# Retention stage of a two-layer backbone kernel: tile records resident in SBUF, scores a step ahead, directions summed in the stage

## The chip, the cores and the metric

The kernel runs on one core of a Trainium2 chip. The metric is the time of one execution on the device in microseconds (us). The engines are named as in the profile: PE (matrix products; PEld its weight loads), DVE (VectorE), ACT (ScalarE), POOL (GpSimd) and SP (SyncE, which here only issues DMAs). Each has its own instruction stream, and they meet through semaphores.

## What is computed

Two layers over 1024 latent and 256 context tokens of width 1024. The change touches the mixer of layer 0 alone: retention in both directions over chunks of 128 tokens, four heads of 128, beside a convolution branch whose normalisation is done in the same stage.

```python
def step(state, qkv):                       # one chunk of 128 tokens, each head
    qc, kc, vc = qkv
    s = jnp.einsum('bhid,bhjd->bhij', qc, kc) * intra
    o = jnp.einsum('bhij,bhjv->bhiv', s, vc) + jnp.einsum('bhid,bhdv->bhiv', qc, state) * xi
    state = state * decay_chunk + jnp.einsum('bhjd,bhjv->bhdv', kc * zeta, vc)
    return state, o
...
oc_f, st_f = retention_chunkwise(qc, kc, vc, lg_f, zero)          # context first
oc_b, st_b = retention_chunkwise(flip(qc), flip(kc), flip(vc), lg_b, zero)
ox_f, _ = retention_chunkwise(qx, kx, vx, lg_f, st_f)             # then the latents
ox_b, _ = retention_chunkwise(flip(qx), flip(kx), flip(vx), lg_b, st_b)
...
ret = head_group_norm(o_f, gn_g) * silu(gf) + head_group_norm(o_b, gn_g) * silu(gb)
conv = conformer_conv(bv, bg, conv_w, conv_b, ln_g, ln_b)
out = concatenate([ret, conv], axis=-1) @ w_out
```

After this come the second norm, an expert-choice mixture (16 experts), and a second layer with latent attention instead of retention.

## The kernel before

The kernel is a chain of stages with a barrier between them: `front` (input projection and convolution), `retention`, `mixer_out` (output projection, norm, router), `routing`, `experts`, then `latents`, `attention`, `mixer_out`, `routing`, `experts` for layer 1. Inside a stage each engine's code is written by hand in order, and semaphores join them; nothing reorders it.

`front` leaves one record per token tile in `rec_d`: turned queries, turned keys, keys, values (128 x 512 fp32 each, so 1 MB) and two gates of 256 KB. Context tiles are stored twice, ahead of and behind the latent ones.

`retention` (L813) runs 10 steps, one tile for each direction d. In step t direction 0 takes record t and direction 1 record 11 - t. One step does, for both directions:

- PE: the scores (L921), a turn of the convolution tile `ys` (L239), keys times values (L932), the outputs (L941 and L942 in turns), a turn of `yn` (L239).
- DVE: mask the scores into `sm` (L978, reads PSUM and SBUF), scale the queries into `qx` (L980, both inputs in SBUF), statistics of the convolution tile (L983, L988), its shift `cnm` (L990), statistics of the outputs (L995, L1000), new state (L1005, PSUM and SBUF), shift `nm` (L1011, SBUF only).
- POOL: reciprocal roots of the convolution tile (L1039, L1043), of each direction (L1047, L1050), the decayed keys `kz` of the next step (L1031), the gate product into `ret` (L1057).
- ACT: `yn` (L1093), the next `ys` (L1086), the normalised outputs `xh` (L1102), the convolution result `mixc` (L1109).
- SP: the records of two steps on (L878, L880) into two buffers per direction, issued when that buffer's gate product is done; then three stores, `mixc` into `mix_d` and the two directions into `ret_f_d` and `ret_b_d` (L892, L897).

All products of a step wait for the step before: `sm`, `qx`, `kz` and `state` have one buffer for each direction. The output weights (4 MB, L869) are loaded ahead of the first record.

`mixer_out` (L1117) takes a tile at a time: SP loads both directions of the tile (L1185, L1186) and the convolution half (L1190), POOL adds the directions (L1351), PE turns the sum, ACT copies it into `mix`, ACT and DVE split `mix` into a high and a low part, PE multiplies (L1254), DVE forms the residual and the norm (L1320 to L1336), PE turns `h` (L239) and routes it (L1277). The first tile also waits for the split weights (L1375, L1378, L1291, L1294); later tiles wait for the rows of modulation (L1308).

Of the kernel before, what the change touches and what calls it, by code (L numbers as in the profile page):

```python
# [25 lines left out]
ALU = mybir.AluOpType  # L26
# [3 lines left out]
P = 128  # L30
# [782 lines left out]
def retention(nc, io, g, conv):  # L813


    with ExitStack() as st:
# [3 lines left out]
        carve = Carve(g.ring, WOUT)  # L820
        rec = [[carve(5 * HALF) for b in range(2)] for d in dirs]
        table = tile("table", [P, 6 * P + 2])
        lg, lga, decay = (tile(n, [P, 2 * HEADS]) for n in ("lg", "lga", "decay"))
        intra = [carve(HALF) for d in dirs]
        xi = [carve(HALF) for d in dirs]
        zeta = tile("zeta", [P, 2 * HEADS])
        state = [carve(HALF) for d in dirs]
        sm = [carve(HALF) for d in dirs]
        qx = [carve(HALF) for d in dirs]
        kz = [carve(HALF) for d in dirs]  # L830
        xh = [carve(HALF) for d in dirs]
        ret = [[tile(f"ret{d}{b}", [P, HALF]) for b in range(2)] for d in dirs]
        stats = [tile(f"stats{d}", [P, HEADS, 6]) for d in dirs]
        mv = [tile(f"mv{d}", [P, HEADS, 2]) for d in dirs]
        ve = [tile(f"ve{d}", [P, HEADS]) for d in dirs]
        rs = [tile(f"rs{d}", [P, HEADS]) for d in dirs]
        nm = [tile(f"nm{d}", [P, HEADS]) for d in dirs]
# [5 lines left out]
        table_in, lg_in, ln_in, setup = sem("table_in"), sem("lg_in"), sem("ln_in"), sem("setup")  # L843
        tables_made = sem("tables_made")
        rec_in = [sem.pair(f"rec_in{d}") for d in dirs]
        ret_out = [sem.pair(f"ret_out{d}") for d in dirs]
        scored = [sem(f"scored{d}") for d in dirs]
        masked = [sem(f"masked{d}") for d in dirs]
        qx_set = [sem(f"qx_set{d}") for d in dirs]
        kz_set = [sem(f"kz_set{d}") for d in dirs]  # L850
        kv_sum = [sem(f"kv_sum{d}") for d in dirs]
        out_sum = [sem(f"out_sum{d}") for d in dirs]
        state_set = [sem(f"state_set{d}") for d in dirs]
        stat = [sem(f"stat{d}") for d in dirs]
        root = [sem(f"root{d}") for d in dirs]
        shift = [sem(f"shift{d}") for d in dirs]
        normed = [sem(f"normed{d}") for d in dirs]
        gated = [sem(f"gated{d}") for d in dirs]
        c_cut, c_turned, c_stat, c_root, c_shift, c_normed, c_back, c_done = (
            sem("c_" + n) for n in ("cut", "turned", "stat", "root", "shift", "normed", "back", "done"))  # L860
        mixc_out = sem.pair("mixc_out")

        with nc.Block() as block:
            @block.sync
            def _(sp):
                sp.dma_start(table[:, :], io["ret_table"]).then_inc(table_in, 16)
                sp.dma_start(lg[:, :], io["ret_logit"].partition_broadcast(P)).then_inc(lg_in, 16)
                sp.dma_start(ln[:, :], io["conv_ln"]).then_inc(ln_in, 16)
                sp.dma_start(g.ring[:, 0:WOUT], io["ev_w_out"]).then_inc(g.wout_in, 16)  # L869
                sp.dma_start(g.router[:, :], io["router_w"][0]).then_inc(g.wout_in, 16)  # L870

                def load(a):
                    for d in dirs:
                        r = a.t if d == 0 else NT + 1 - a.t
                        sp.wait_ge(gated[d], a.t + 1)
                        settle(sp, g)
                        src = rows(io["rec_d"], r)
                        sp.dma_start(rec[d][a.b][:, 0:4 * HALF], src[:, 0:4 * HALF]).then_inc(rec_in[d][a.b], 16)  # L878
                        gcol = (R_GF + d) * HALF
                        sp.dma_start(rec[d][a.b][:, 4 * HALF:], src[:, gcol:gcol + HALF]).then_inc(rec_in[d][a.b], 16)  # L880
                for d in dirs:
                    sp.sem_inc(ret_out[d][0], 16)
                    sp.sem_inc(ret_out[d][1], 16)
                sp.sem_inc(mixc_out[0], 16)
                sp.sem_inc(mixc_out[1], 16)

                def step(a):
                    if a.plus(2).exists(NT):
                        load(a.plus(2))
                    sp.wait_ge(c_done, a.t + 1)  # L890
                    settle(sp, g)
                    sp.dma_start(rows(io["mix_d"], a.t)[:, HALF:D], mixc[a.b][:, :]).then_inc(mixc_out[a.b], 16)  # L892
                    for d in dirs:
                        r = a.t if d == 0 else NT + 1 - a.t
                        sp.wait_ge(gated[d], a.t + 3)
                        settle(sp, g)
                        sp.dma_start(rows(io["ret_d"][d], r), ret[d][a.b][:, :]).then_inc(ret_out[d][a.b], 16)  # L897
                load(At(0, 0))
                load(At(0, 1))
                run(sp, step, NT // 2, 0, NT // 2 - 1)  # L900
                for b in range(2):
                    sp.wait_ge(mixc_out[b], 16 * (NT // 2 + 1))
                    for d in dirs:
                        sp.wait_ge(ret_out[d][b], 16 * (NT // 2 + 1))

            @block.tensor
            def _(pe):
                for d in dirs:
                    pe.sem_inc(kv_sum[d], 1)
                    pe.sem_inc(out_sum[d], 1)  # L910

                def hs(x, h, at=0):
                    return x[:, at + h * HD:at + (h + 1) * HD]
# [1745 lines left out]
```

## Time and profile before

| | |
|---|---|
| three runs | 3379.59, 3380.14 (median), 3390.08 us |
| profiled execution | 3382.69 us, its span 3380.9 us |
| PE, DVE, ACT, POOL busy | 2924.2, 2080.8, 1409.5, 520.6 us |
| retention, first DMA to that of the next stage | 513.3 to 673.1 us |
| mixer_out of layer 0 | 673.1 to 856.5 us |
| mean granted TensorE clock | 0.935 of full speed |

The page shows shares of the whole span. The touched stage is 160 us of 3381, so it is read from the timeline, from the busy time by stretch, and from the waits inside it. A row of the timeline gives start, duration, engine, line, operation, output and inputs, and in brackets the idle time before it with what ended it.

### The profile page before, as it was taken

To read this page: it belongs to the slowest core of one execution; us is meant where nothing else is said; L and a number is where in the kernel's file an instruction comes from. 1 tells how busy PE (TensorE), PEld (TensorE's weight loads), DVE (VectorE), ACT (ScalarE), POOL (GpSimd) and SP (SyncE) were. 2 spreads that over 40 slices of the span, in tenths; PEclk is the share of its full clock that TensorE was granted. 3 is DMA by queue.
4 is the path that set the end of the run, shared out by engine and by line. 5 is a ranking of instruction groups with operands and counts; after the bars stand their busy time and mean duration, and the time that the engine had idled before them with its cause. 6 is when DMAs were issued, how large, how long until landed. Compare 5 with 4: busy or idle time off the path is not lost. (4 is left out here: it accounts for less than half of the span.)

```text
span 3380.9 us, 51489 instructions
## 1 busy us (share of the span) xinstructions
PE 2924.2 (86%) x19792; PEld 2312.1 (68%) x19792; DVE 2080.8 (62%) x2164; ACT 1409.5 (42%) x1717; POOL 520.6 (15%) x487
## 2 busy tenths in 40 slices
PE   6999995688099999999949997799997819999998
PEld 3766785667078888888835554688886708777776
DVE  3577825654766666666712232566664488888887
ACT  2212114432055555555512334344332217777675
POOL 0000004511012122212214446000000001111111
PEclk8999997899599999999979999899998959999999
DMA  5368616653467788778641223522203349999995
GB/s 214 125 211 267 218 60 250 221 184 128 171 224 279 284 308 283 280 284 304 222 167 45 69 66 95 157 81 61 70 21 112 119 183 359 377 375 373 370 378 174
DMA packets 160338, 690.25 MB, mean 204 GB/s; under 512 B 14337, under 2 KB 78849, under 8 KB 124514
## 3 DMA queue, kind: packets, MB, share of 16 engines
q1 hardware_dynamic: 145634, 650.97, 52.8%
q0 software_dynamic: 14592, 37.76, 4.7%
q8 instruction: 73, 1.20, 0.1%
q14 instruction: 39, 0.32, 0.0%
HBM read 600.50 MB, written 88.18 MB: 204 GB/s over the span
## 5 line engine op out<-in xcount | busy, mean ns | idle before, releaser
L1784 DVE TENSOR_TENSOR ex_wlo<-ring,ex_whi 128x2048 fp32r<-128x2048 f32 x384 | 877.2, 2289 | 264.9 <-ACT ex_whi L1711 260.8
L1711 ACT CAST ex_whi<-ring 128x2048 fp32r<-128x2048 f32 x384 | 727.5, 1905 | 251.1 <-PE psum L1676 250.8
L1676 PE MATMUL psum<-ex_whi,ex_xh 128*128 128x512 f32 x1024 | 411.4, 402 | 10.8 <-DVE ex_wlo L1784 10.8
L1676 PE MATMUL psum<-ex_wlo,ex_xh 128*128 128x512 f32 x1024 | 401.2, 392 | 0.0
L1676 PE MATMUL psum<-ex_whi,ex_xl 128*128 128x512 f32 x1024 | 400.8, 391 | 0.0
L1676 PEld LDWEIGHTS psum<-ex_whi,ex_xh 128*128 128x128 f32 x1024 | 193.5, 189 | 61.6 <-DVE ex_wlo L1784 14.8
L529 PE MATMUL psum<-fr_whi,fr_hh 128*128 128x512 f32 x560 | 223.8, 401 | 12.9 <-DVE fr_hl L713 11.5
L1676 PEld LDWEIGHTS psum<-ex_whi,ex_xl 128*128 128x128 f32 x1024 | 193.4, 189 | 41.8
L1676 PEld LDWEIGHTS psum<-ex_wlo,ex_xh 128*128 128x128 f32 x1024 | 193.7, 189 | 37.2
L529 PE MATMUL psum<-fr_wlo,fr_hh 128*128 128x512 f32 x560 | 218.1, 391 | 0.7 <-DVE fr_wlo L719 0.7
L529 PE MATMUL psum<-fr_whi,fr_hl 128*128 128x512 f32 x560 | 218.1, 391 | 0.0
L1676 PE MATMUL psum<-ex_whi,ex_hh 128*128 128x512 f32 x512 | 211.1, 412 | 0.0
L1676 PE MATMUL psum<-ex_whi,ex_hl 128*128 128x512 f32 x512 | 202.2, 395 | 0.0
L1676 PE MATMUL psum<-ex_wlo,ex_hh 128*128 128x512 f32 x512 | 201.9, 394 | 0.0
L774 DVE SCALAR_TENSOR_TENSOR conv_y<-conv_u,fr_taps,conv_y 128x1295 f32<-128x1295 f32 x120 | 180.0, 1560 | 0.0
L2438 PE MATMUL psum<-ring 128*128 128x128 f32 x1280 | 161.5, 282 | 7.2 <-DVE ring L2450 6.0
L2438 PEld LDWEIGHTS psum<-ring 128*128 128x128 f32 x1280 | 149.4, 193 | 18.2 <-DVE ring L2450 13.9
L2034 PE MATMUL psum<-ring,la_cT 128*128 128x384 f32 (+1 forms) x416 | 154.0, 530 | 0.6 <-ACT la_cT L2108 0.6
L1574 POOL DMA_INDIRECT x_d<-ring,idx_x x16 | 52.5, 3281 | 608.4 <-DVE ring L1822 608.4
L239 PE MATMUL psum<-ident,ring 128*128 128x128 f32 x440 | 64.9, 294 | 82.2 <-DMA ring<-h_d,idx_x 39.4
L529 PEld LDWEIGHTS psum<-fr_whi,fr_hh 128*128 128x128 f32 x560 | 105.6, 189 | 40.9 <-DVE fr_hl L713 11.9
L1254 PE MATMUL psum<-mo_w_high,mo_mix_high 128*128 128x512 f32 x288 | 118.2, 410 | 17.7 <-DVE mo_mix_low L1299 17.7
(278 smaller groups left out, 5235.8 us busy)
## 6 DMA issues: line engine op xcount, KB each, us to landing
ring<-in_moe_w SPq DMA_DIRECT2D x192, 2048.0 KB, 9.8
fr_raw<-in_mod_w SPq DMA_DIRECT2D x40, 1024.0 KB, 5.7
ring<-rec_d SPq DMA_DIRECT2D x20, 1024.0 KB, 7.1
rec_d<-fr_work SPq DMA_DIRECT2D x72, 256.0 KB, 5.8
fr_raw<-in_ev_w_in SPq DMA_DIRECT2D x14, 1024.0 KB, 5.6
h_d<-ring SPq DMA_DIRECT2D x18, 512.0 KB, 3.0
fr_arena<-in_mod_w SPq DMA_DIRECT2D x8, 1024.0 KB, 13.8
ring<-mod_d SPq DMA_DIRECT2D x11, 512.0 KB
```

Source lines behind the costliest of these rows:

```text
L239: last = nc.tensor.transpose(g.psum[:, bank + n // 4, (n % 4) * P:(n % 4 + 1) * P], src[:, k * P:(k + 1) * P], g.ident[:, :])
L529: last = nc.tensor.matmul(g.psum[:, bank(s), :], pairs[n][0][t][:, 4 * b + k, :], pairs[n][1][m % 3][:, k, :], start=(b == 0 and i == 0), ...
L774: nc.vector.scalar_tensor_tensor(conv.y[:, j, :], us, w, conv.y[:, j, :], ALU.mult, ALU.add).then_inc(conv_set[j], 1)
L1254: last = nc.tensor.matmul(g.psum[:, 1 + 2 * a.b + c, :], x_part[a.b][:, k * P:(k + 1) * P], w_part[:, k, c * BANK:(c + 1) * BANK], start=( ...
L1574: pool.indirect_dma_start(dst, bass.IndirectOffsetOnAxis(ap=idx[:, e:e + 1], axis=0), src[:, :], None, compute_op=ALU.add).then_inc(done, 16)
L1676: last = nc.tensor.matmul(g.psum[:, 2 + i % 2, :], x[:, 4 * b + k, :], w[n][:, k, :], start=(b == 0 and k == 0 and first == 0), stop=(b == ...
L1711: nc.scalar.copy(whi[m % RING][:, :, :], slot(i)[:, 4 * b:4 * b + 4, :]).then_inc(hi_set, 1)
L1784: nc.vector.tensor_tensor(wlo[n][:, :, :], slot(i)[:, 4 * b:4 * b + 4, :], whi[n][:, :, :].bitcast(F32), ALU.subtract).then_inc(lo_set, 1)
L2034: last = nc.tensor.matmul(g.psum[:, 6 + m % 2, 0:width], cT[:, (k0 + k) * P:(k0 + k + 1) * P], w[:, k, c0:c0 + width], start=(k == 0), sto ...
L2438: last = nc.tensor.matmul(g.psum[:, 7, 0:P], v[mu // per_head_units][:, k, :], pT[:, k * P:(k + 1) * P], start=(k == 0), stop=(k == KEYT - 1))
```

## The change

- The records of all ten tiles stay in the ring, 1 MB each, loaded once; context records serve both directions. Only gates are still double buffered (L872), freed by the gate product. They fill the first 10 MB of the 14 MB ring, so the output weights' place is taken by the first four slots, and the weights come in two halves of 2 MB, after steps 2 and 7 (L898 to L905), when those tiles are finished in both directions.
- `sm`, `qx` and `state` have two buffers. The masked scores of step i + 1 are made at the head of step i on DVE, and PE computes scores i + 1 ahead of everything else of step i.
- On DVE the state update moves ahead of the statistics; the shift of direction 1 moves into the next step. On ACT direction 1 is normalised at the head of the next step. On POOL the gate products follow a step behind, and the decayed keys come before the roots of the directions.
- The gate product of the direction that reaches a tile first is written into `total`; the other multiplies in place (L1084) and adds (L1088). `total` lies where the convolution input was. One store per tile goes to `mix_d`. In `mixer_out` the two loads and the add become one load (L1250).
- The loops are written out, so branches, tick increments and register waits go; SP loads `re_lg` ahead of the table.

```diff
+        order = [[XT, XT + 1] + list(range(XT)), [XT + 1, XT] + list(reversed(range(XT)))]
+        slots = [8, 9, 3, 4, 0, 7, 1, 6, 2, 5]
+        rec = {t: g.ring[:, n * TREC:(n + 1) * TREC] for n, t in enumerate(slots)}
+        total = [uf[:, t * HALF:(t + 1) * HALF] for t in range(NT)]
+        def second(i):
+
+            return i == 1 or i >= 2 + XT // 2
...
+                for i in range(2, 2 + XT // 2):
+                    for d in dirs:
+                        load_rec(order[d][i])
...
+                    if i == 2:
+                        for d in dirs:
+                            sp.wait_ge(out_sum[d], 2)
+                        load_wout(0)
...
+                for i in range(NT):
+                    if i + 1 < NT:
+                        for d in dirs:
+                            scores(i + 1, d)
...
+                def gated_output(i, d):
+                    b, t = i % 2, order[d][i]
+                    pool.wait_ge(normed[d], i + 1)
+                    pool.wait_ge(gate_in[d][b], 16 * (i // 2 + 1))
+                    if not second(i):
+                        nc.gpsimd.tensor_tensor(total[t], xh[d][:, :], gate[d][b], ALU.mult).then_inc(gated[d], 1)
+                        return
+                    nc.gpsimd.tensor_tensor(xh[d][:, :], xh[d][:, :], gate[d][b], ALU.mult).then_inc(gated[d], 1)
...
+                    nc.gpsimd.tensor_tensor(total[t], total[t], xh[d][:, :], ALU.add).then_inc(added[d], 1)
...
-                        rt = a.t - XT if a.stream() else a.t + CT
-                        sp.dma_start(rf[b], rows(io["ret_d"][0], rt)).then_inc(r_in[b], 16)
-                        sp.dma_start(rb[b], rows(io["ret_d"][1], a.t + CT)).then_inc(r_in[b], 16)
+                        sp.dma_start(ret[b], rows(io["mix_d"], a.t)[:, 0:HALF]).then_inc(r_in[b], 16)
...
-                def add(a):
-                    pool.wait_ge(r_in[a.b], 32 * (a.i + 1))
-                    pool.wait_ge(r_turned, a.t + 1)
-                    nc.gpsimd.tensor_tensor(rsum, rf[a.b], rb[a.b], ALU.add).then_inc(r_sum, 1)
```

DVE, one step of retention before: masks, convolution statistics, output statistics, state, with a shift behind each state.

```order
180 L978 TENSOR_TENSOR ring<-psum,ring 128x512
181 L980 TENSOR_TENSOR ring<-ring 128x512
182 L978 TENSOR_TENSOR ring<-psum,ring 128x512
183 L980 TENSOR_TENSOR ring<-ring 128x512
184 L983 BN_STATS re_cst<-psum 128x6
185 L988 BN_AGGR re_cmv<-re_cst 128x2
186 L990 SCALAR_TENSOR_TENSOR re_cnm<-re_cmv,re_crs 128x1
187 L995 BN_STATS re_stats<-psum 128x6 x4
188 L1000 BN_AGGR re_mv<-re_stats 128x2 x4
```

DVE, after, from the shift of direction 0 that closes one step: the masks that follow serve the outputs of the step after the one they stand in; the second shift belongs to the step just closed.

```order
197 L1032 SCALAR_TENSOR_TENSOR re_nm<-re_mv,re_rs 128x4
198 L1001 TENSOR_TENSOR ring<-psum,ring 128x512
199 L1002 TENSOR_TENSOR re_qx<-ring 128x512
200 L1032 SCALAR_TENSOR_TENSOR re_nm<-re_mv,re_rs 128x4
201 L1001 TENSOR_TENSOR ring<-psum,ring 128x512
202 L1002 TENSOR_TENSOR re_qx<-ring 128x512
203 L1044 BN_STATS re_cst<-psum 128x6
204 L1048 BN_AGGR re_cmv<-re_cst 128x2
205 L1012 SCALAR_TENSOR_TENSOR re_state<-re_state,re_decay,psum 128x128 x4
206 L1054 SCALAR_TENSOR_TENSOR re_cnm<-re_cmv,re_crs 128x1
207 L1012 SCALAR_TENSOR_TENSOR re_state<-re_state,re_decay,psum 128x128 x4
```

The masks moved a step ahead, a state update came between the statistics and `cnm`, and the output statistics moved to the step's end.

POOL, one step before: roots of the directions, then keys, then both gate products.

```order
47 L1050 TENSOR_TENSOR re_rs<-re_ve,mhalf 128x4
48 L1047 TENSOR_SCALAR re_ve<-re_mv 128x4
49 L1050 TENSOR_TENSOR re_rs<-re_ve,mhalf 128x4
50 L1031 TENSOR_TENSOR ring<-ring,re_zeta 128x512 x2
51 L1057 TENSOR_TENSOR re_ret<-ring 128x512 x2
```

POOL, one step after in which the tiles are met for the second time (L1084 the product, L1088 the add).

```order
99 L1084 TENSOR_TENSOR ring<-ring 128x512
100 L1088 TENSOR_TENSOR conv_u<-conv_u,ring 128x512
101 L1109 TENSOR_SCALAR re_cve<-re_cmv 128x1
102 L1113 TENSOR_TENSOR re_crs<-re_cve,mhalf 128x1
103 L1073 TENSOR_TENSOR ring<-ring,re_zeta 128x512 x2
104 L1084 TENSOR_TENSOR ring<-ring 128x512
105 L1088 TENSOR_TENSOR conv_u<-conv_u,ring 128x512
```

The keys now follow the convolution's root at once, and one gate product lies on each side of them; the roots of the directions come last.

## Rows read from the trace of the kernel before

**Rows 1.** Busy time by stretch, from one `cnm` to the next. Columns: stretch, length, PE, PEld, DVE, ACT, POOL (instructions), clock, DMA share, GB/s.
```profile
540.08:552.53 12.45, 11.05 (x98) 10.78 (x97) 9.18 (x34) 7.08 (x15) 8.72 (x10) 1.00 0.12 34
...
552.53:565.89 13.36, 8.37 (x47) 7.76 (x47) 9.21 (x33) 5.70 (x14) 7.83 (x10) 0.74 0.82 289
...
sum 118.11, PE 88.91 PEld 85.30 DVE 82.96 ACT 52.41 POOL 75.03; mean PE 9.88 PEld 9.48 DVE 9.22 ACT 5.82 POOL 8.34
```

**Rows 2.** Groups of instructions, 540 to 660 us: busy, mean ns, idle before.
```profile
L921 PE MATMUL psum<-ring 128*128 128x128 f32 x144 | 25.1, 330 | 26.6 <-DMA ring<-rec_d 26.6
```

**Rows 3.** Timeline of one step, ACT, POOL and DVE, 623 to 631 us.
```profile
623.53 1.03 POOL L1050 TENSOR_TENSOR re_rs<-re_ve,mhalf 128x4 f32<-128x4 f32 x1
623.94 0.15 DVE L1011 SCALAR_TENSOR_TENSOR re_nm<-re_mv,re_rs 128x4 f32<-128x4 f32 x1
...
624.13 3.00 ACT L1102 ACTIVATE ring<-psum,re_nm,re_rs 128x128 f32<-128x128 f32 x8 [3.46 <-DVE re_nm L1011]
624.53 2.15 POOL L1031 TENSOR_TENSOR ring<-ring,re_zeta 128x512 f32<-128x512 f32 x2
625.05 0.54 DVE L1011 SCALAR_TENSOR_TENSOR re_nm<-re_mv,re_rs 128x4 f32<-128x4 f32 x1
...
626.64 3.40 POOL L1057 TENSOR_TENSOR re_ret<-ring 128x512 f32<-128x512 f32 x2
...
630.43 0.58 POOL L1043 TENSOR_TENSOR re_crs<-re_cve,mhalf 128x1 f32<-128x1 f32 x1
```

**Rows 4.** Line L980 (`qx`) in the whole stage: duration ns least, median, most.
```profile
L980 DVE TENSOR_TENSOR ring<-ring x20: 680/888/1459, 534.2 to 654.7; 128x512 f32<-128x512 f32 x20
```

**Rows 5.** Timeline of the stage's start, DVE, PE and POOL.
```profile
526.69 1.29 DVE L968 TENSOR_TENSOR ring<-ring,re_table 128x512 f32<-128x512 f32 x2 [6.22 <-ACT re_decay L1078]
...
531.46 2.07 PE L921 MATMUL psum<-ring 128*128 128x128 f32 x8 [22.88 <-DMA ring<-rec_d]
...
543.34 1.05 POOL L1050 TENSOR_TENSOR re_rs<-re_ve,mhalf 128x4 f32<-128x4 f32 x1
```

**Rows 6.** Timeline of PE: keys times values at either clock, outputs, turn.
```profile
640.05 1.95 PE L932 MATMUL psum<-ring 128*128 128x128 f32 x16
...
641.84 0.39 PE L941 MATMUL psum<-ring 128*128 128x128 f32 x2
...
645.41 0.60 PE L239 MATMUL psum<-ident,re_yn 128*128 128x128 f32 x4
...
654.74 3.23 PE L932 MATMUL psum<-ring 128*128 128x128 f32 x16
```

**Rows 7.** Timeline of the stage's end, POOL and SP's queue.
```profile
663.51 1.04 POOL L1050 TENSOR_TENSOR re_rs<-re_ve,mhalf 128x4 f32<-128x4 f32 x1
...
665.70 2.67 POOL L1057 TENSOR_TENSOR re_ret<-ring 128x512 f32<-128x512 f32 x2 [1.16 <-ACT ring L1102]
...
669.42 0.39 SPq L897 DMA_DIRECT2D ret_b_d<-re_ret  x1
673.10 0.35 SPq L1173 DMA_DIRECT2D mo_gn<-in_ret_gn_g  x1
```

**Rows 8.** Timeline in `mixer_out`, DVE and POOL.
```profile
693.66 2.36 DVE L1308 SCALAR_TENSOR_TENSOR ring<-ring 128x1024 f32<-128x1024 f32 x2 [4.21 <-DMA ring<-in_norm_g]
...
703.67 1.29 POOL L1351 TENSOR_TENSOR ring<-ring 128x512 f32<-128x512 f32 x1
703.74 2.30 DVE L1333 SCALAR_TENSOR_TENSOR ring<-ring,mo_rstd 128x1024 f32<-128x1024 f32 x1 [2.25 <-POOL mo_rstd L1362]
...
830.11 1.29 DVE L1333 SCALAR_TENSOR_TENSOR ring<-ring,mo_rstd 128x1024 f32<-128x1024 f32 x1 [2.15 <-POOL mo_rstd L1362]
```

**Rows 9.** Timeline of PE in `mixer_out`: turns of `h` for tiles 7 and 8.
```profile
818.23 1.09 PE L239 MATMUL psum<-ident,ring 128*128 128x128 f32 x8 [1.11 <-DVE ring L1336]
...
832.71 1.09 PE L239 MATMUL psum<-ident,ring 128*128 128x128 f32 x8
```

**Rows 10.** Waits, 700 to 860 us: us in total, times, longest.
```profile
PE psum L239 <- DVE ring L1336: 16.8, 9, 5.7
```

More of the change, by code:

```diff
@@ new lines, in scores @@
+                def scores(i, d):
+                    r = rec[order[d][i]]
+                    pe.wait_ge(rec_in[order[d][i]], 16)
+                    if i:
+                        pe.wait_ge(masked[d], i)
+                    for h in range(HEADS):
+                        last = nc.tensor.matmul(g.psum[:, d, h * P:(h + 1) * P], hs(r, h, R_KT * HALF),
+                                                hs(r, h, R_QT * HALF), start=True, stop=True)
+                    last.then_inc(scored[d], 1)
@@ new lines, in update @@
+                def update(i, d):
+                    dve.wait_ge(kv_sum[d], i + 1)
+                    if i:
+                        dve.wait_ge(out_sum[d], i)
+                    dve.wait_ge(state_set[d], i + 1)
+                    for h in range(HEADS):
+                        c = slice(h * P, (h + 1) * P)
+                        last = nc.vector.scalar_tensor_tensor(state[d][(i + 1) % 2][:, c], state[d][i % 2][:, c],
+                                                              decay[:, d * HEADS + h:d * HEADS + h + 1],
+                                                              g.psum[:, 2 + d, c], ALU.mult, ALU.add)
+                    last.then_inc(state_set[d], 1)
@@ new lines, in moments @@
+                def moments(i, d):
+                    dve.wait_ge(out_sum[d], i + 1)
+                    if i:
+                        dve.wait_ge(root[d], 2 * i - 1)
+                        dve.wait_ge(shift[d], i)
+                    for h in range(HEADS):
+                        nc.vector.bn_stats(stats[d][:, h, :], g.psum[:, 4 + d, h * P:(h + 1) * P]).then_inc(stat[d], 1)
+                    dve.wait_ge(stat[d], 2 * HEADS * i + HEADS)
+                    for h in range(HEADS):
+                        nc.vector.bn_aggr(mv[d][:, h, :], stats[d][:, h, :]).then_inc(stat[d], 1)
@@ L971, in _, with shifted @@
+                def shifted(i, d):
+                    dve.wait_ge(root[d], 2 * i + 2)
+                    if i:
+                        dve.wait_ge(normed[d], i)
+                    nc.vector.scalar_tensor_tensor(nm[d][:, :], mv[d][:, :, 0], -1.0, rs[d][:, :],
+                                                   ALU.mult, ALU.mult).then_inc(shift[d], 1)
                 for d in dirs:
-                    dve.sem_inc(masked[d], 1)
-                def step(a):
+                    mask(0, d)
@@ new lines, in normalise @@
+                def normalise(i, d):
+                    act.wait_ge(shift[d], i + 1)
+                    if i:
+                        act.wait_ge(gated[d], i)
+                        if second(i - 1):
+                            act.wait_ge(added[d], seconds(i - 1))
+                    for h in range(HEADS):
+                        c = slice(h * P, (h + 1) * P)
+                        last = nc.scalar.activation(xh[d][:, c], g.psum[:, 4 + d, c], ACT.Identity,
+                                                    bias=nm[d][:, h:h + 1], scale=rs[d][:, h:h + 1])
+                    last.then_inc(normed[d], 1)
```

400 lines of the change are left out of this document (189 added, 211 removed).

## The prediction

> **What bounds the kernel now.** The stages follow each other behind barriers, so the question is what retention (513.3 to 673.1 us) and the `mixer_out` behind it (to 856.5) cost; nothing after them starts earlier by itself, and what is gained there shortens the whole. I read first the busy time from one `cnm` to the next [rows 1]: nine steps take 118.1 us, 13.1 each, while PE is busy 9.9, DVE 9.2, POOL 8.3 and ACT 5.8. No engine is full. Then the waits: PE waits for records 26.6 us in nine steps, 3.0 each [rows 2]. But the first stretch, which moves next to nothing by DMA, still takes 12.45 us [rows 1]. So the records explain some 0.7 to 3 us of a step, and a ring of dependent work the rest: roots on POOL, shift on DVE, eight normalisations on ACT (3.00 us), and only then outputs, keys and gate products [rows 3]. Its order, more than its content, is what the change alters.
>
> A third thing is to be seen there. An operation of DVE with two inputs in SBUF is held up by a POOL operation on 512 columns: the shift `nm` takes 0.15 us alone and 0.54 beside `kz`, ending when the first `kz` does [rows 3]; `qx` takes 0.68 to 1.46 us [rows 4]; and in `mixer_out` L1333 takes 2.30 us when POOL's add starts 0.07 ahead of it, 1.29 without an add [rows 8]. Beside POOL's root (L1050) the shift kept its 0.15 [rows 3].
>
> **The change, part by part.**
>
> *Retention, a step without adds.* I count from the end of the root of direction 0 on POOL (0.0). DVE: shift at 0.0, first mask with `qx` to 1.5, shift of direction 1 to 1.65 (POOL's second root takes 1.4), second `sm` to 2.3. ACT has direction 0 normalised at 1.75 (half of 3.00), so POOL's gate product starts at 2.0 and holds the second `qx` until 3.3: it ends at 3.9. Convolution statistics to 4.9, POOL's root of them to 6.0 (0.58 for the power [rows 3]). POOL goes on to `kz` without a gap, and `cnm`, with two SBUF inputs, loses to it as L1333 lost to the add, which followed a root in the same way [rows 8]: `cnm` ends at 7.1. One state update has run meanwhile, the other ends at 8.2, the statistics of direction 0 at 9.6, POOL's sum and root 1.5 later. A step is thus 11.2 us. As a check on DVE's busy time: 9.2 [rows 1], less 0.4 of the held `nm` and 0.4 to 0.6 of two `qx` (median 0.89, least 0.68 [rows 4]), is 8.3; about 0.75 of small waits between dependent operations (an estimate), 1.05 for the second `qx`, 0.9 for `cnm` and 0.2 until the root give 11.2.
>
> The other engines have room. PE at full clock needs 1.95 for the scores, as many columns as L932, 1.95 for keys, 3.6 for the outputs (641.84 to 645.41) and two turns of about 0.5 [rows 6]: 8.5 us, waiting some 2.5. POOL has 8.3, ACT 5.8 [rows 1]. The records: 10.5 MB of records and 1 MB of gates are loaded at the rate at which the start already loads, some 400 GB/s; the pair for step 2 is there more than 10 us ahead. So the 3.0 us of waits [rows 2] go to nothing, and what is late next is DVE.
>
> *Steps with adds.* The add runs in steps 2, 7, 8, 9 and the tail, for both directions. An add is like L1351, 1.29 us [rows 8]; the L1057 product is 1.25 to 1.7 [rows 3, 7]. In steps 2 and 7 POOL is the last: gates 2.0 to 4.7, 0.6 given to `qx`, root 0.9, keys 2.1 (2.15 [rows 3]), gates 2.7, root 1.35, in all 12.3. Step 8 makes no keys: 11.5. Step 9 has no mask, no state: 9.9. Sum: five steps of 11.2 (1, 3 to 6), 2 x 12.3, 11.5, 9.9: **102.0 us**. Before, from the first root's end (544.39 [rows 5]) to the same point of step 9 (its direction 0 ended at about 662.7, 0.8 ahead of the second's start at 663.51 [rows 7]) it was 118.3.
>
> *The start.* The masks wait for `intra`, which ended at 527.98 [rows 5]; its logits are loaded 0.4 earlier now, so 527.6. Before, the first scores waited for a record until 531.46 [rows 5], since 4 MB of weights went first. Now they are ready. From 527.6: first mask 0.7; scores of step 1 at half clock, 2.07 each [rows 5], the second pair from the second mask (530.1), to 532.3; turn 1.0; keys 3.2 at half clock [rows 6] to 536.6; outputs of direction 0 to 538.6; statistics and root 3.2: 541.8. Before it was 544.4: **2.5 us** gained.
>
> *The tail.* Before, the store that ended last was issued at 669.42 and the next stage's first DMA at 673.10, 3.7 later [rows 7]. Now both gate products with adds stand behind the last roots: root of direction 1 to 1.4, products and adds 1.9 to 7.1. So 541.8 + 102.0 = 643.8, + 7.1 + 0.1 + 3.7 = 654.7. Against 673.1 retention gains **18.4 us**. The weights are there: their second half is issued after step 7, over 25 us ahead of use, and 2 MB are some 5 us of DMA. Gates are asked for a whole step early.
>
> *mixer_out.* Two loads and an add leave each tile. The add had no place on the path by itself, but it holds L1333: 2.30 against 1.29 [rows 8], 1.01 us in each of eight tiles, and PE then waits for L1336 behind it, 16.8 us in 9 waits, one of 5.7 in the last tile, so 11.1 in the other eight, the least 1.1 [rows 9, 10]. Each wait is longer than what DVE saves, so all of 8 x 1.01 = **8.1 us** comes off. The tile after the last add took 14.5 us with PE waiting for nothing [rows 9]; that is the floor. At the start, the rows of modulation and the norm's gain, landed at 693.66 [rows 8], hold tile 1; 0.5 MB less lies ahead of them, **1.3 us**. Bounds: 0 and 10.
>
> All in all 18.4 + 8.1 + 1.3 = 27.8 us. The profiled execution took 3382.7 (span 3380.9): 3354.9. It was 2.6 above the median of the runs, which I take as the scatter of runs; against the median, **3352**.
>
> **A rule weighed.** The Trainium skill, SBUF — State Buffer, "Who interferes with whom", says that a DVE instruction with two SBUF inputs and a POOL instruction that reads SBUF exclude each other for the whole instruction, the first to start winning. The L1333 and `nm` rows agree. It would also hold `nm` beside POOL's root, which also reads SBUF; there the row has 0.15, so the measurement decides.
>
> **Rivals.**
>
> *A, ports dearer.* If the roots also hold DVE, the first `qx` waits from 0.9 to 1.4, and POOL, held in turn, slips as L1057 does (1.70 a piece beside `qx`, 1.33 later [rows 3, 7]): 0.5 to 1.0 more a step. Or the steps stay at the 12.45 that a step without DMA took [rows 1]: 9 x 12.45 = 112, 10 more, 3362. For: DVE and POOL overlap more than before. Against: the order is another.
>
> *B, ports cheaper.* If `cnm` and `qx` win their races, 1.95 a step goes where DVE is last, six steps: 12 less, but POOL's own round (first gate product from 2.0, root, keys, second product, root) then closes the step at about 10, so 8 or 9 less: 3343.
>
> *C, the clock, slower than before.* At the stage's start the scores run at half speed, and in steps of 13.4 us with a waiting PE the mean granted clock was 0.74 [rows 1]. Keys then cost 3.23 instead of 1.95 [rows 6]; at that ratio PE needs 8.5 x 1.66 = 14.1, with turns and waits some 16, in every step: nine steps 144 us, 42 more, 3394. It decides from 14.3 us a step, where the gain of 28 is spent. For: the stretch of 552.53 had it in part. Against: it fell when PE had waited for records, and stayed at 1.00 through the stretch with PE busy 11.05 of 12.45 [rows 1]; now it is about 8.5 of 11.2.
>
> *D, the change brings the records but not the rest.* If the ring of POOL, DVE and ACT closes as before and the add's removal is taken up by another wait, only 2.5 at the start and about 1 a step of waits remain, less 2 in the tail: 3371.
>
> **How the numbers follow.** Forecast (3346 to 3358) 0.55; A at its far end 0.17; B 0.13; D 0.08; C 0.05; anything else 0.02. The range is 3340 to 3367: it leaves out C, D and the rest, and takes in B and A with a few us for the mixer's bound. A measurement of this kernel can tell about 0.3%, 10 us, from no change. Below 3370: forecast, A, B and part of D, 0.89. Within: the rest of D, 0.05. Slower: C and half of the rest, 0.06.
>
> **What would show it.** Right: `cnm` to `cnm` of 11.2 us, and 12.3 in steps 2 and 7; no PE wait for `rec_d` after the first scores; `cnm` at about 1 us instead of 0.16 behind L1113; `qx` of direction 1 at 1.5; L1333's successor at 1.29 in all tiles, mixer tiles of 14.5; the stage's length 141 us. Wrong: steps of 12.5 with POOL full say A; 10 with `cnm` at 0.16 says B; a clock near 0.5 in mid-stage says C; a new PE wait in `mixer_out`, for the copied sum or the split, says that the 8.1 was not free. A wait for a gate or for the weights would break the sum at a place where I gave nothing.

## The result, and the profile after

The changed kernel takes 3348.23 us (median of five runs, 3343.91 to 3358.16) against 3380.14 us for the kernel before (five runs, 3377.04 to 3390.08): ratio 0.9903, 95% interval 0.988 to 0.9926. The forecast of 3352 (3340 to 3367) held. Its profiled execution took 3348.23 us, span 3344.6, against 3382.69 and 3380.9. That the total lay so near is partly luck: in the traces the two stages gained 11 us more than forecast, and 7 us of that gain is not seen in the medians. So the result is laid out by stage.

| profiled execution, us | before | after | difference | forecast |
|---|---|---|---|---|
| all ahead of retention | 513.3 | 512.1 | -1.3 | 0 |
| retention, first DMA to the next stage's | 159.8 | 131.2 | -28.6 | -18.4 |
| mixer_out of layer 0 | 183.4 | 172.9 | -10.5 | -9.4 |
| all behind it | 2524.4 | 2528.5 | +4.1 | 0 |

Busy time by stretch in the kernel after, from one `cnm` to the next, as [rows 1]. Columns: stretch, length, PE, PEld, DVE, ACT, POOL (instructions), clock, DMA share, GB/s.

```profile
565.98:576.12 10.14, 8.48 (x74) 8.12 (x73) 9.70 (x35) 5.73 (x14) 7.84 (x11) 1.00 0.61 204
576.12:586.36 10.24, 8.57 (x74) 8.14 (x73) 9.75 (x34) 5.73 (x14) 7.93 (x11) 1.00 0.24 79
...
606.84:618.61 11.77, 9.88 (x72) 9.69 (x72) 9.72 (x33) 5.73 (x14) 10.72 (x13) 0.86 0.60 204
...
sum 95.11, PE 76.34 PEld 73.56 DVE 83.44 ACT 52.71 POOL 77.20; mean PE 8.48 PEld 8.17 DVE 9.27 ACT 5.86 POOL 8.58
```

Nine steps take 95.1 us where they took 118.1. DVE's busy time is what it was, 9.3 a step; the step has closed up around it. PE waits for a record only ahead of the first scores (waits of 510 to 660 us: total, times, longest), where [rows 2] had 26.6 us inside the steps.

```profile
PE psum L930 <- DMA ring<-rec_d: 12.9, 2, 12.5
```

The start, PE's timeline. The first scores run at half clock as in [rows 5], but start 7.7 us after the stage's first DMA instead of 18.1. The granted clock had risen when the keys came: L938 takes 1.95 us, where the forecast had 3.2.

```profile
519.81 2.08 PE L930 MATMUL psum<-ring 128*128 128x128 f32 x8 [12.49 <-DMA ring<-rec_d]
522.34 2.02 PE L930 MATMUL psum<-ring 128*128 128x128 f32 x8 [0.46 <-DMA ring<-rec_d]
527.07 3.59 PE L930 MATMUL psum<-ring 128*128 128x128 f32 x16 [2.71 <-DVE ring L1001]
...
531.17 1.95 PE L938 MATMUL psum<-ring 128*128 128x128 f32 x16
```

The end, SP's queue, as [rows 7]: the tail from the root of direction 0 in the last step (632.90) to the next stage is 10.3 us, as before.

```profile
637.48 2.89 SPq L917 DMA_DIRECT2D mix_d<-conv_u  x2
643.23 0.35 SPq L1239 DMA_DIRECT2D mo_gn<-in_ret_gn_g  x1
```

`mixer_out`: L1397 (L1333 before) at all its 18 places, least, median and most in ns; PE's first product and three turns of `h`; PE's waits for the line behind L1397 (L1400, L1336 before), 650 to 818 us.

```profile
L1397 DVE SCALAR_TENSOR_TENSOR ring<-ring,mo_rstd x18: 1283/1284/1286, 673.7 to 2659.2; 128x1024 f32<-128x1024 f32 x18
```
```profile
653.19 0.79 PE L1318 MATMUL psum<-mo_w_high,mo_mix_high 128*128 128x512 f32 x1 [5.39 <-DVE mo_mix_low L1363]
...
690.66 1.09 PE L239 MATMUL psum<-ident,ring 128*128 128x128 f32 x8
...
705.24 1.09 PE L239 MATMUL psum<-ident,ring 128*128 128x128 f32 x8 [0.18 <-DVE ring L1400]
...
719.72 1.09 PE L239 MATMUL psum<-ident,ring 128*128 128x128 f32 x8
```
```profile
PE psum L239 <- DVE ring L1400: 7.6, 5, 5.7
```

Nothing holds L1397 any more, the tiles are 14.5 us apart, and of the 16.8 us of waits in [rows 10] the last tile's 5.7 and little more are left. The first product comes 9.96 us after the stage's first DMA, before 12.0, but that brings little: the rows of modulation that tile 1 waits for (L1372, L1308 before) are used 20.4 us after the first DMA instead of 20.6, and the first L1397 starts at 30.5 instead of 30.6.

### The profile page after: what moved, and what is told of

The parts are those of the page before. It is cut to its first block and busy times, and to the rows that moved or that the text cites. A ratio compares the mean times of both kernels' runs of the same rounds, so it can differ in the third digit from the quotient of the medians.

```text
span 3344.6 us, 51073 instructions
## 1 busy us (share of the span) xinstructions
PE 2917.5 (87%) x19776; PEld 2305.3 (69%) x19776; DVE 2074.1 (62%) x2156; ACT 1409.5 (42%) x1717; POOL 513.8 (15%) x485
## 5 line engine op out<-in xcount | busy, mean ns | idle before, releaser
L1731 PE MATMUL psum<-ex_whi,ex_xh 128*128 128x512 f32 x1024 | 410.8, 401 | 10.8 <-DVE ex_wlo L1839 10.8
L1629 POOL DMA_INDIRECT out_x<-ring,idx_x x16 | 52.3, 3271 | 513.8 <-DVE ring L1877 513.8
```

The costliest lines, as they stand in the source:

```text
L1629: pool.indirect_dma_start(dst, bass.IndirectOffsetOnAxis(ap=idx[:, e:e + 1], axis=0), src[:, :], None, compute_op=ALU.add).then_inc(done, 16)
L1731: last = nc.tensor.matmul(g.psum[:, 2 + i % 2, :], x[:, 4 * b + k, :], w[n][:, k, :], start=(b == 0 and k == 0 and first == 0), stop=(b == ...
```

## A step read from the other end

The forecast read steps from one `cnm` to the next and found 12.45 us in a stretch with little DMA [rows 1]. From the end of one root of direction 0 (L1050) to the next, the same trace of the kernel before reads differently:

```profile
544.39:555.55 11.16, 7.82 (x65) 7.12 (x64) 9.44 (x39) 7.08 (x15) 8.69 (x10) 1.00 0.40 138
555.55:570.54 14.99, 11.95 (x80) 11.69 (x80) 8.94 (x30) 5.69 (x14) 7.84 (x10) 0.77 0.84 284
570.54:581.75 11.21, 7.73 (x66) 7.18 (x64) 9.47 (x39) 5.60 (x14) 8.69 (x10) 1.00 0.66 234
581.75:597.55 15.80, 13.08 (x80) 12.72 (x80) 8.94 (x31) 5.70 (x14) 7.83 (x10) 0.68 0.80 273
```

Short and long steps alternate. In the long ones PE waits twice for records (1.57 and 2.81 us, then 1.88 and 2.22) and its clock falls; in the third line it still waits once, 2.01 us; in the first it waits for none. The nine steps took 11.16, 14.99, 11.21, 15.80, 11.23, 13.99, 12.65, 11.69 and 15.64 us. So the old order was good for about 11.2 us, not 12.45; without any wait for records it takes 10.8, as the first experiment shows. The stretch of 12.45 us began in the start-up step: its part up to the root took 4.31 us, with PE busy throughout, where the next one took 3.02. The experiments below use this measure ("root to root").

## The experiments

**Records resident, order as before.** The kernel before with resident records, gates in buffers of their own, the weights in two halves and the loops written out. Its order on every engine, its single buffers, its two stores, and the loads and the add of `mixer_out` stay.

```diff
-        rec = [[carve(5 * HALF) for b in range(2)] for d in dirs]
+        slots = [8, 9, 3, 4, 0, 7, 1, 6, 2, 5]
+        store = {t: g.ring[:, n * TREC:(n + 1) * TREC] for n, t in enumerate(slots)}
+        gate = [[carve(HALF) for b in range(2)] for d in dirs]
...
-                sp.dma_start(g.ring[:, 0:WOUT], io["ev_w_out"]).then_inc(g.wout_in, 16)
...
+                load_rec(XT)
+                load_rec(XT + 1)
+                load(At(0, 0))
+                load(At(0, 1))
+                for t in (0, 7, 1, 6, 2, 5, 3, 4):
+                    load_rec(t)
```

> The kernel before with only the records resident: all ten loaded once, the output weights in two halves behind them, the retention loops written out; order of work on every engine, single buffers, two stores, the add in mixer_out as before. Theory (the gain of a step comes from the order as well as from the loads): the steps fall from 13.1 us only to about 12.0 to 12.4, the wait for records to nothing, the start gains 4; the stage goes from 159.8 to about 147, and the kernel gains 11 to 13 us of the 32. Rival (record loads were the cost): steps of 10.2 to 10.6, the stage at about 133.

Median 3362.51 us (3358.41 to 3366.63, four runs), ratio 0.9928 (0.991 to 0.9946). The stage takes 133.1 us (513.02 to 646.10), `mixer_out` 183.1. So 26.7 of the 28.6 us that retention gained are here, without the new order. The expectation (steps of 12.0 to 12.4, a stage of 147) missed; its rival was right on the stage. Root to root, two of the eight steps that took 10.8:

```profile
560.46:571.27 10.81, 8.60 (x74) 8.14 (x74) 9.09 (x34) 5.69 (x14) 8.68 (x10) 1.00 0.39 134
571.27:582.09 10.82, 8.62 (x75) 8.16 (x74) 9.10 (x34) 5.69 (x14) 8.69 (x10) 1.00 0.90 306
```

Nine steps take 97.7 us (118.4 before, 94.4 in the changed kernel). The second line loads at 306 GB/s and is no longer than the first. The rest of the change to the stage (order, second buffers, the sum made in the stage, one store) is worth 3.3 us in nine steps, and gives back 1.0 at the start (first root 26.4 us after the stage's first DMA, here 25.5) and 0.4 in the tail.

**Loops written out, nothing else.** The kernel before with all ten steps of the stage written out. The cut shows SP; the other four engines have the same edit.

```diff
-                run(sp, step, NT // 2, 0, NT // 2 - 1)
+                run(sp, step, NT // 2, NT // 2, 0)
```

> The kernel before with the retention loops written out and nothing else. Theory (branches, ticks and register waits cost a little in every step): DVE's and POOL's hand-offs inside a step shrink, steps of 12.4 to 12.8 us instead of 13.1, the stage 3 to 6 us shorter than 159.8. Rival (they lie beside other work): 13.0 to 13.2.

One run, 3394.88 us; the stage takes 156.6, 3.2 less. The first step, which waits for no record, takes 11.15 us (11.16 before), and the third, in which PE waits once, 11.17 (11.21 before):

```profile
578.31:589.48 11.17, 7.73 (x66) 7.18 (x64) 9.45 (x39) 5.68 (x14) 8.69 (x10) 1.00 0.63 224
```

So ticks and branches cost at most 0.05 us a step. The 3.2 us lie in the start (0.6) and in the steps that wait longer for records, whose pattern differs between the two traces. The whole is longer than before because in this execution what stands ahead of the stage took 521.6 us instead of 513.3, and what stands behind `mixer_out` 2531.3 instead of 2524.4.

**Output weights behind the first records.** The kernel before with one load moved.

```diff
-                sp.dma_start(g.ring[:, 0:WOUT], io["ev_w_out"]).then_inc(g.wout_in, 16)
-                sp.dma_start(g.router[:, :], io["router_w"][0]).then_inc(g.wout_in, 16)
...
                 load(At(0, 0))
                 load(At(0, 1))
+                sp.dma_start(g.ring[:, 0:WOUT], io["ev_w_out"]).then_inc(g.wout_in, 16)
+                sp.dma_start(g.router[:, :], io["router_w"][0]).then_inc(g.wout_in, 16)
```

> The kernel before, with the load of the output weights and of the router issued behind the records of steps 0 and 1 instead of ahead of them. Theory (the 5.6 us that the start gained with resident records come from the first scores not waiting behind 4 MB): first root of direction 0 ends 25.5 to 27 us after the stage's first DMA instead of 31.05; the nine steps stay at 116 to 120, the stage at 154 to 156 instead of 159.8. Rival (the gain comes from the records' own number or from the order): 30 to 31 at the first root, stage 159 to 160.

One run, 3370.76 us. The first root ends 25.7 us after the first DMA instead of 31.05, the nine steps stay at 117.9, and the stage takes 154.0, 5.8 less. PE waits for no record any more; both scores start right behind DVE's tables, which end at 525.19:

```profile
525.40 3.75 PE L920 MATMUL psum<-ring 128*128 128x128 f32 x16 [19.48 <-DVEq L971]
```

This settles the start: the 4 MB ahead of the first record cost 5.4 us, which two moved lines give back. The nine steps shorten by the other 20.7 us only when the records are resident.

**The hold of `cnm`.** In the changed kernel `cnm` takes 0.89 to 1.21 us beside the keys, where it took 0.16. Here its second input is a scalar for each partition.

```diff
-                    nc.vector.scalar_tensor_tensor(cnm[:, :], cmv[:, 0:1], -1.0, crs[:, :],
-                                                   ALU.mult, ALU.mult).then_inc(c_shift, 1)
+                    nc.vector.tensor_scalar(cnm[:, :], cmv[:, 0:1], crs[:, 0:1], -1.0,
+                                            ALU.mult, ALU.mult).then_inc(c_shift, 1)
```

> The changed kernel with one edit: cnm is made by a tensor_scalar that takes the root as a scalar, so it has one tensor input in SBUF instead of two. Theory (the operation with two inputs in SBUF is held by POOL's first key product): cnm takes 0.16 us instead of 0.99, and each step in which DVE is last shortens by about 0.8 us, from 10.2 to 9.4; in steps 2 and 7, where POOL is last, nothing. Six steps: the stage 131 us minus some 5. Rival (cnm is long because the root's result arrives late): it stays at about 1 us and the steps at 10.2.

One run, 3362.26 us. The hold is gone:

```profile
L1054 DVE TENSOR_SCALAR re_cnm<-re_cmv,re_crs x10: 206/214/214, 543.4 to 636.9; 128x1 f32<-128x1 f32 x10
```

Root to root stays at 10.10 us (10.14 in the changed kernel), the stage takes 129.7 instead of 131.2, of which 0.9 are step 8, where no keys are made. So the hold, 0.8 us on DVE in each step, had slack to stand in, and the 5 us expected from its removal did not come. Only in step 8 (10.67 us, here 9.74) does it cost: there POOL has no keys to make, and in the changed kernel waits 0.99 us for DVE's statistics. What closes the other steps is seen on POOL:

```profile
594.27 0.23 POOL L1109 TENSOR_SCALAR re_cve<-re_cmv 128x1 f32<-128x1 f32 x1 [1.46 <-DVE re_cmv L1048]
594.59 0.58 POOL L1113 TENSOR_TENSOR re_crs<-re_cve,mhalf 128x1 f32<-128x1 f32 x1
595.13 2.04 POOL L1073 TENSOR_TENSOR ring<-ring,re_zeta 128x512 f32<-128x512 f32 x2
...
597.13 1.28 POOL L1082 TENSOR_TENSOR conv_u<-ring 128x512 f32<-128x512 f32 x1
...
598.49 0.23 POOL L1094 TENSOR_SCALAR re_ve<-re_mv 128x4 f32<-128x4 f32 x1
...
598.80 1.03 POOL L1098 TENSOR_TENSOR re_rs<-re_ve,mhalf 128x4 f32<-128x4 f32 x1
```

POOL waits 1.46 us for the convolution statistics, then works without a gap to the root, 5.56 us. DVE takes 4.4 us from the root before (589.76) to the statistics' end (594.18). 4.4 + 5.6 is the step, a ring through both engines, and the held `qx` (1.49 us) stands in DVE's part of it. DVE ended the statistics of direction 0 at 597.75 and the root began only at 598.49, behind the gate product.

**Both second holds.** The same, and `qx` of direction 1 right behind that of direction 0, ahead of the second shift.

```diff
+                    if d == 0:
+                        scaled_queries(i, 0)
+                        scaled_queries(i, 1)
```

> The changed kernel with cnm from a tensor_scalar (one tensor input in SBUF) and the second qx ahead of the second shift and mask, so that it runs before POOL's gate product starts. Theory (two held operations cost 0.8 and 0.9 us a step where DVE is last): qx 0.68 in all places, cnm 0.16, steps from 10.2 to about 9.1 to 9.4 until POOL's own round is last, steps 2 and 7 at about 11; the stage 6 to 9 us shorter than 131.2, the kernel 0.2 to 0.3% faster than the changed one. Rival (another wait is right behind): less than 2 us.

Median 3354.01 us (3347.81 to 3358.36, four runs), ratio 0.9909 (0.9893 to 0.9926). `qx` is free, two in 1.28 us, but now the shift `nm` behind it meets the gate product, and PE no longer gets its masks sooner. Two lines of DVE:

```profile
582.73 1.28 DVE L1011 TENSOR_TENSOR re_qx<-ring 128x512 f32<-128x512 f32 x2
583.93 1.23 DVE L1041 SCALAR_TENSOR_TENSOR re_nm<-re_mv,re_rs 128x4 f32<-128x4 f32 x1
```

Root to root 10.20 us, the stage 130.6; the expected 6 to 9 us did not come, and the rival (less than 2) was right. Here the hold only moved to the next operation with two inputs in SBUF. The convolution statistics still end about 4.5 us after the root, and the step is as long.

**The convolution statistics earlier.** If the ring is DVE's way to these statistics and then POOL's row, it must shorten when they move. First with the one-input `cnm`, then with `cnm` as in the changed kernel:

```diff
                         if d == 0 and i:
                             shifted(i - 1, 1)
+                        if d == 0:
+                            dve.wait_ge(c_turned, i + 1)
+                            nc.vector.bn_stats(cst[:, :], g.psum[:, 6, :]).then_inc(c_stat, 1)
...
+                            nc.vector.bn_aggr(cmv[:, :], cst[:, :]).then_inc(c_stat, 1)
```

> The changed kernel with cnm of one SBUF tensor input, and with the statistics of the convolution tile taken between the two masks of the step instead of behind both. Theory (the step closes through POOL: convolution statistics on DVE at +4.4, then root, keys, the second gate product and the root of direction 0 in a row on POOL, 5.6 us, so 10.1 in all, and DVE's own ring is only 9.1): root to root 9.1 to 9.4 us in steps without adds instead of 10.1, 10.8 to 11 in steps 2 and 7 instead of 11.75 (POOL is then busy without a gap), stage 122 to 125 us instead of 129.7 in the kernel with one-input cnm alone. Rival (DVE's or PE's own ring closes the step): root to root stays at 10.1 and the stage at 129 to 131.

> The same move of the statistics, but cnm with its two SBUF inputs as in the changed kernel. Theory (the hold of cnm by the keys cost nothing where it stood, since DVE had slack, and costs as soon as DVE's ring closes the step): root to root 9.7 to 10.0 us, about 0.6 more than with the one-input cnm; if the hold is never on the ring, the same 9.1 to 9.4 as there; if the statistics' place is not what closes the step, 10.1.

With one-input `cnm`: median 3346.94 us (3337.49 to 3355.97, five runs), ratio 0.989 (0.9861 to 0.992). Root to root 9.04 us, the stage 125.1, so the ring was the right one. With the held `cnm` (one run, 3353.83): 9.08, the stage 127.1; 0.9 of these 2.0 us are step 8 again. The first kernel's lines, a step without adds and step 7, and two of the operations in the former:

```profile
583.67:592.69 9.02, 8.42 (x74) 8.10 (x73) 8.03 (x33) 5.72 (x14) 8.14 (x10) 1.00 0.28 89
601.73:613.47 11.74, 9.76 (x84) 9.22 (x82) 8.12 (x33) 5.71 (x14) 10.69 (x12) 1.00 0.35 106
```
```profile
585.47 1.27 POOL L1083 TENSOR_TENSOR conv_u<-ring 128x512 f32<-128x512 f32 x1 [0.39 <-ACT ring L1158]
...
586.61 0.68 DVE L1002 TENSOR_TENSOR re_qx<-ring 128x512 f32<-128x512 f32 x1
```

POOL no longer waits for the convolution statistics (1.46 us before); from this gate product it works without a gap up to the root at 592.69. The 9.04 us are POOL's own round, with only 0.39 of waiting for ACT. The move did two things at once. It took the second mask and `qx` from in front of the statistics, and it freed that `qx`: it starts 0.13 us before POOL's product ends and takes 0.68 instead of 1.49 us. What each is worth was not tested apart.

Two expectations missed. Steps 2 and 7 did not move: POOL's 10.69 us of work, about 0.08 of hand-off behind each operation and 0.39 of waiting for ACT are already 11.74. And outside step 8 the held `cnm` costs next to nothing still (0.81 here), since POOL reaches the root of direction 0 just as DVE has the statistics (592.63):

```profile
591.32 1.27 POOL L1083 TENSOR_TENSOR conv_u<-ring 128x512 f32<-128x512 f32 x1
592.72 0.23 POOL L1095 TENSOR_SCALAR re_ve<-re_mv 128x4 f32<-128x4 f32 x1
```

**An add, or a fill, in `mixer_out`.** The changed kernel with an addition on POOL of the size and place of the one removed, whose result nobody uses, and the same with a fill of that tile.

```diff
+                    if even and a.plus(1).exists(nt):
+                        pool.wait_ge(a_made, streams)
+                        nc.gpsimd.tensor_tensor(extra, arow[0][:, 0:HALF], arow[0][:, HALF:D], ALU.add)
```
```diff
+                        nc.gpsimd.memset(extra, 0.0)
```

> The changed kernel with an add of 128x512 put back on POOL in mixer_out at the place of the old one; nobody waits for its result and it reads rows that are there anyway. Theory (the old add cost by holding DVE's operation with two inputs in SBUF): that operation takes 2.30 us again in the tiles with an add instead of 1.28, PE waits 1.1 us or more for the turn of h, mixer_out grows by 8 us from 172.9 to 181. Rival (the gain came from the load and the shorter chain of add and turn): it stays at 172.9.

> As the run with the add put back, but the POOL operation is a fill of 128x512, which reads nothing from SBUF. Theory (only POOL operations that read SBUF hold DVE): DVE's operation keeps 1.28 us and mixer_out 172.9. Rival (any POOL operation of that size holds it, or POOL's time itself counts): 2.0 us or more and mixer_out 178 or more.

With the add (one run, 3362.95 us) `mixer_out` takes 182.5, with the fill (one run, 3353.44) 172.7, in the changed kernel 172.9. POOL and DVE, with the add and with the fill:

```profile
707.00 1.29 POOL L1416 TENSOR_TENSOR ring<-ring 128x512 f32<-128x512 f32 x1
```
```profile
707.07 2.30 DVE L1398 SCALAR_TENSOR_TENSOR ring<-ring,mo_rstd 128x1024 f32<-128x1024 f32 x1 [2.15 <-POOL mo_rstd L1423]
```
```profile
706.02 0.53 POOL L1416 MEMSET ring<- 128x512 f32 x1
```
```profile
706.11 1.28 DVE L1398 SCALAR_TENSOR_TENSOR ring<-ring,mo_rstd 128x1024 f32<-128x1024 f32 x1 [2.16 <-POOL mo_rstd L1423]
```

```profile
L1398 DVE SCALAR_TENSOR_TENSOR ring<-ring,mo_rstd 128x1024 f32<-128x1024 f32 x10 | 21.0, 2100 | 21.6 <-POOL mo_rstd L1423 21.6
```

The last line is the group of L1398 in the kernel with the add, ten of 2.10 us on the mean, 8.2 us more than the 12.8 without it. The add alone, with nobody waiting for its result, costs 9.6 us, and PE's waits behind L1401 return to 16.1 (7.7 with the fill). The fill starts at the same place ahead of L1398, overlaps it, and holds nothing.

The 9.6 us are not all hold. From the first L1398 to the second, the kernel with the add takes 16.98 us at a mean granted clock of 0.90, with PE busy for 14.55; the one with the fill 14.38 us at 1.00, with PE busy for 12.92. So 1.6 us of this interval are PE at the lower clock: behind the add PE had waited 2.43 us for L1401, behind the fill 1.46, and then its products came 0.43 us apart instead of 0.23 for a while. The later seven intervals are each about 1.0 us longer. The drop does not always follow: in the kernel before it is there (16.98 us, 0.90), in the one with the weights behind the first records, which also has the add, it is not (15.40 us, 1.00), and that kernel's `mixer_out` takes 181.2 us instead of 183.4.

**The changed kernel again.**

> The changed kernel once more, beside the others of this call. Retention 131.2 us and mixer_out 172.9 as before, to 0.3 us; the stretch behind mixer_out (2528.5 us, 4 more than in the trace of the kernel before) moves by some us from run to run if it is scatter, and stays 4 above that of the kernel before if the change caused it.

Median 3356.48 us (3339.97 to 3364.72, four runs), ratio 0.992 (0.9897 to 0.9944). Stage 131.5 and `mixer_out` 172.6: both repeat within 0.4 us. The kernels with the add and the fill, whose retention is the same, have 132.0 and 132.4 for the stage, so up to 1.2 us between two stages is scatter; root to root repeats within 0.03 us in steps 2 to 9. What stands ahead (510.9) and behind (2521.9) does not repeat. Over the twelve traces the part ahead takes 510.7 to 521.9 us. The part behind takes 2523.1 to 2531.3 in the four kernels with the old order and the old `mixer_out` (mean 2526.5), and 2521.9 to 2534.5 in the other eight (mean 2530.4). The ranges overlap, but the means are 4 us apart, and in routing and experts of layer 0 alone the two groups do not meet (867.6 to 868.2 us against 868.3 to 869.6). The +4.1 of the table is 0.5 in routing and experts, 2.3 in latents, 3.3 in attention with its `mixer_out`, and -2.0 in the last stretch; in this second trace latents and attention are within 1.1 us of the kernel before.

## Why the prediction was right, and where it was wrong

- **Loads off the path: right in kind, its size too small.** The waits went to nothing. The step that failed is "the records explain some 0.7 to 3 us of a step, and a ring of dependent work the rest. Its order, more than its content, is what the change alters". Its first half holds: residency took 20.7 us from nine steps, 2.3 a step. Its second half fails: residency without the order gives 26.7 of 28.6 us, all the rest of the change 1.9, and the old ring of dependent work takes 10.8 us, not 12.45. The cause was the measure: the stretch of 12.45 us between two `cnm` lay across the start-up step and the first full one. The result is in one respect rival D: loads bring nearly all. But D's price for them, "about 1 a step", was 2.3.
- **A step without adds: 11.2 forecast, 10.14 measured,** five steps, 5.2 us. `cnm` (0.99) and the second `qx` (1.49) were held as said, each 0.8 us above its free time (the terms were 0.9 and 1.05). Mis-sized were DVE's busy time, 10.25 by the forecast's terms and 9.70 measured, and its idle time, 0.95 (with the "0.75 of small waits", an estimate with no row) and 0.44 measured. DVE's state updates were to end at 8.2 and the statistics of direction 0 at 9.6 after the root; they ended at 7.5 and 8.7. And "what is late next is DVE" is only half right: DVE sets when POOL's row starts, at 4.5 us, but at the step's end the root of direction 0 stands behind POOL's gate product as much as behind DVE's statistics. One step of the changed kernel, POOL and DVE:

```profile
580.82 0.16 DVE L1032 SCALAR_TENSOR_TENSOR re_nm<-re_mv,re_rs 128x4 f32<-128x4 f32 x1 [0.28 <-POOL re_rs L1098]
...
581.18 1.03 POOL L1098 TENSOR_TENSOR re_rs<-re_ve,mhalf 128x4 f32<-128x4 f32 x1
581.51 0.68 DVE L1002 TENSOR_TENSOR re_qx<-ring 128x512 f32<-128x512 f32 x1
...
582.93 1.49 DVE L1002 TENSOR_TENSOR re_qx<-ring 128x512 f32<-128x512 f32 x1
...
585.07 0.18 DVE L1048 BATCH_NORM_AGGREGATE re_cmv<-re_cst 128x2 f32<-128x6 f32 x1
...
586.36 0.89 DVE L1054 SCALAR_TENSOR_TENSOR re_cnm<-re_cmv,re_crs 128x1 f32<-128x1 f32 x1
...
588.19 1.27 POOL L1082 TENSOR_TENSOR conv_u<-ring 128x512 f32<-128x512 f32 x1
...
589.11 0.38 DVE L1026 BATCH_NORM_AGGREGATE re_mv<-re_stats 128x2 f32<-128x6 f32 x4
...
589.58 0.23 POOL L1094 TENSOR_SCALAR re_ve<-re_mv 128x4 f32<-128x4 f32 x1
```

  The statistics end at 589.49, POOL's product at 589.46: a tie, so taking 0.8 from DVE left 10.10. Rival B's number, a step of about 10, came true, but not its reason: `cnm` and `qx` lost their races. The 10.1 us are a ring, 4.5 us of DVE with the held `qx` in it and 5.7 of POOL; POOL's own round, once it no longer waited for the convolution statistics, took 9.04.
- **Steps with adds: 12.3 forecast, 11.74 and 11.75 measured.** POOL closes them, as said; the 0.6 was given to a held POOL that lost only 0.3. Step 8 took 10.67 (11.5), step 9 9.41 (9.9). All nine: 94.4 against 102.0.
- **The start: 2.5 forecast, 4.6 measured.** The mechanism was right, shown with the weights moved alone. The size missed because keys were priced at half clock (3.2 instead of 1.95) and turns with them.
- **The tail: 10.9 forecast, 10.3 measured.** As before the change.
- **The clock (rival C).** It stayed at 1.00 in every stretch up to step 7, then 0.86 and 0.72 in the last two, and the steps there were no longer for it: POOL closed them. In the kernel before it had been 0.68 to 0.87 in the five steps of 12.6 us and more, in which PE waited for records, and 1.00 in the four shorter ones.
- **mixer_out: 9.4 forecast, 10.5 measured.** The add put back costs 9.6 us. The hold is the 8.2 by which L1398 grows in all, as forecast (8.1). The term of 1.3 for the start failed: the rows of modulation were used 0.2 us earlier, and the first L1397 started 0.2 us earlier. In its place stand 1.6 us of PE at the lower clock in the first interval, which the forecast did not have, and 0.4 in the second; with them the number came out near.
- **The rule weighed.** It holds for `cnm`, `qx` and L1398 in these runs, and the forecast was right to set it aside beside POOL's root. In the changed kernel `nm` no longer meets that root, but `qx` of direction 0 does: in all nine steps it starts 0.3 us after L1098, lies inside its 1.03 us, and keeps 0.68 us. So the premise of rival A, that roots hold DVE too, did not come true.
- **The total.** The stages gained 39.1 us in the traces, 11 more than the 27.8 forecast. The medians differ by 31.9 and, in the second comparison, 28.0. So 7 to 11 us of what the stages gained is not seen in the medians. Parts that the change does not touch scatter by 10 us from run to run, and that alone could explain it. But the mean of the part behind is 4 us longer in the eight traces of changed kernels than in the four others, so some of it may be a lasting loss; the cause was not looked for. Against the sum by stage the forecast was too low, and its total lay near by luck, since it had neither the extra gain of the stages nor the loss in the medians.

## What to carry to other kernels

Measure a pipeline's step between two ends of the same operation on the engine that closes it, and look at each step apart: a mean over alternating 11 and 15 us hid that waits for loads were nearly the whole case. A held operation costs only what sticks out of the ring that closes the step; find that ring by the engine that works without a gap up to the closing operation, and move what starts its row. Freeing a held operation inside the ring may bring nothing when the next one is held in its place. For an engine's add that nobody waits for, ask which operation of the neighbour it holds.

The best version found is the changed kernel with the convolution statistics between the masks and a one-input `cnm`: 6.1 us less in retention than the changed kernel by the traces, at a median of 3346.94 us too near to 3348.23 and 3356.48 to be told apart by the medians. Steps 2 and 7 are then POOL's alone.

## What the runs showed of the hardware

- An operation on one column, `cnm`, 0.16 us alone, was held to 0.89 to 1.21 us beside POOL's 128 x 512 product when it read two tensors in SBUF; as a `tensor_scalar` whose second operand is a scalar for each partition it took 0.21 us in the same place. The Trainium skill, SBUF — State Buffer, "Who interferes with whom", speaks of instructions with two SBUF inputs; the runs show that this scalar does not count as one.
- POOL's fill of 128 x 512, 0.53 us, held L1398 not at all (1.28); the add of the same size did (2.30).
- Statistics of a PSUM tile and the state update, which reads PSUM and SBUF, ran beside POOL's products unheld. In the kernel with the statistics moved, the statistics (L1045) took 0.69 us beside the gate product, and 0.69 in the kernel with one-input `cnm` alone, where they lie clear of it; the state update (L1012) took 1.11 us for four beside the keys, and 1.11 ahead of them.
- POOL's root of 128 x 4 (L1098, 1.03 us), which reads SBUF, did not hold `qx` of 128 x 512, which has two inputs in SBUF and started 0.3 us later: 0.68 us in nine steps of nine.
- In these rows the hold cost the later starter only: POOL's product kept its 1.27 to 1.28 us while `qx` was held, and POOL's `re_cve`, started 0.2 us after a `qx`, was held to 0.55 instead of 0.23 us in the kernels with the statistics moved.
